# Prompt experts: ScalarE weights the V row, GpSimd adds it to a sum in SBUF, and the token rows stand in PSUM

## What is computed

```python
def peer_ffn(h, w_q, sub_keys, u_tab, v_tab):
    def one(hb):                       # a block of 128 tokens
        ...                            # scores against keys, the best 16 of each of 8 heads
        gate = jax.nn.softmax(best_s, axis=-1)
        act = jax.nn.gelu(jnp.einsum('thkd,td->thk', u_tab[idx], hb), approximate=False)
        return jnp.einsum('thk,thkd->td', gate * act, v_tab[idx])

x = x + g2 * peer_ffn(hff, ...)
```

## Time and profile before

| | |
|---|---|
| median of 3 runs | 4979.95 us (4967.22 to 4985.87) |
| the profiled execution | 4967.69 us |
| its span, first to last instruction | 4965.9 us |
| from the first dot of the prompt's slots to the last, within the span | 393 to 1103 us in layer 0, 2824 to 3529 us in layer 1 |

### The profile page before, as it was taken

How to read it: one execution, slowest core, us unless ns; L and a number is a source line. 1 busy time by engine, 2 the same in 40 slices (tenths; PEclk the granted TensorE clock), 3 DMA queues, 4 the chain that set the end, 5 groups by cost and what they waited for, 6 DMA issues and landing times. The chain is left out here.

```text
span 4965.9 us, 36487 instructions
## 1 busy us (share of the span) xinstructions
PE 3861.3 (78%) x11046; PEld 1898.0 (38%) x11046; DVE 3242.6 (65%) x8263; ACT 748.0 (15%) x2211; POOL 1447.9 (29%) x1284
## 2 busy tenths in 40 slices
PE   7588678988777776788868786788977687777776
PEld 6464334643222222235535443346422222222222
DVE  1546765536887868854574766664378787687666
ACT  0111124211101010010121112341010100100101
POOL 0001112212454434432222021221044354354432
PEclk9788788999999999999989897899999999999999
DMA  8334456754998999999969254566389899899998
GB/s 266 99 116 178 153 188 242 252 194 192 412 415 368 421 374 414 421 390 387 365 245 366 97 203 146 206 253 220 127 354 421 365 419 421 362 421 421 407 421 341
DMA packets 342149, 1497.72 MB, mean 302 GB/s; under 512 B 31424, under 2 KB 176448, under 8 KB 178112
## 3 DMA queue, kind: packets, MB, share of 16 engines
q0 software_dynamic: 184320, 1342.26, 67.4%
q1 hardware_dynamic: 157632, 153.13, 9.6%
HBM read 1491.97 MB, written 3.31 MB: 301 GB/s over the span
## 5 line engine op out<-in xcount | busy, mean ns | idle before, releaser
L680 PE MATMUL expert_acc<-uv_ring,diag 128*128 128x512 f32 x3744 | 1865.1, 631 | 417.9 <-DVE diag L1227 407.8
L634 POOL DMA_INDIRECT uv_ring<-uv,expert_index x936 | 1050.2, 1122 | 2717.1 <-PE expert_acc L680 2174.4
L680 PEld LDWEIGHTS expert_acc<-uv_ring,diag 128*128 128x128 f32 x3744 | 688.1, 198 | 1487.8 <-DVE diag L1227 898.5
L1218 DVE CUSTOM_DVE_ANT_0 uv_ring<-uv_ring,arena 128x1024 f32<-128x1024 f32 x680 | 831.5, 1223 | 243.2 <-DMA uv_ring<-uv,expert_index 240.5
L680 PE MATMUL expert_acc<-arena,diag 128*128 128x512 f32 x1376 | 687.8, 632 | 264.2 <-DVE diag L1227 196.3
L951 ACT ACTIVATE gelu<-u_dot 128x1 f32<-128x1 f32 x1280 | 256.0, 203 | 2943.8 <-DVE u_dot L1218 2943.2
L1227 DVE TENSOR_SCALAR diag<-const_mats,expert_gate,gelu 128x128 f32<-128x128 f32 x1280 | 465.7, 364 | 308.8 <-ACT gelu L951 214.1
L634 POOL DMA_INDIRECT arena<-uv,expert_index x344 | 397.6, 1156 | 757.2 <-PE expert_acc L680 460.3
L1218 DVE CUSTOM_DVE_ANT_0 arena<-arena 128x1024 f32<-128x1024 f32 x344 | 420.8, 1223 | 172.6 <-DMA arena<-uv,expert_index 171.2
L680 PEld LDWEIGHTS expert_acc<-arena,diag 128*128 128x128 f32 x1376 | 243.4, 195 | 698.1 <-DVE diag L1227 425.2
L1218 DVE CUSTOM_DVE_ANT_0 uv_ring<-uv_ring,prompt_rows 128x1024 f32<-128x1024 f32 x256 | 312.1, 1219 | 113.4 <-DMA uv_ring<-uv,expert_index 112.9
(11 more groups left out here) (202 smaller groups left out, 2785.0 us busy)
## 6 DMA issues: line engine op xcount, KB each, us to landing
w_ring<-w_ada SPq DMA_DIRECT2D x66, 512.0 KB, 11.3
w_ring<-w_in SPq DMA_DIRECT2D x64, 512.0 KB, 5.0
w_ring<-w_pq SPq DMA_DIRECT2D x64, 512.0 KB, 4.5
w_ring<-w_out SPq DMA_DIRECT2D x32, 512.0 KB, 6.3
uv_ring<-w_ada SPq DMA_DIRECT2D x30, 512.0 KB, 5.3
uv_ring<-uv,expert_index POOLq DMA_INDIRECT x936, 11.7
arena<-b_ada SPq DMA_DIRECT2D x48, 128.0 KB, 6.2
arena<-uv,expert_index POOLq DMA_INDIRECT x344, 15.7
```

Source lines behind the costliest of these rows:

```text
L634: pool.indirect_dma_start(out=UV[j], out_offset=None, in_=uv, in_offset=bass.IndirectOffsetOnAxis(ap=idxs[:, n % 2, k:k + 1], axis=0)).the ...
L680: ins = pe.matmul(acc[:, half, :], diag[:, m % DIAGS, :], UV[SLOT_AT[m]][:, D + 512 * half:D + 512 * half + 512], start=(k == 0), stop=(k ...
L1218: V_.tensor_tensor_reduce(UV[j][:, 0:D], UV[j][:, 0:D], rows_of(n), 1.0, 0.0, ALU.mult, ALU.add, dots[:, m % DOTS:m % DOTS + 1]).then_inc( ...
```

## The change

For the two prompt blocks only (`summed_by_pool(n)`, n = 0 and 5), steps 3 to 5 above are done by other engines:

- ScalarE, after the gelu, multiplies it with the gate (a 128x1 instruction), and then multiplies the whole v row of 1024 in place with that number (a 128x1024 instruction), at the same point of its program as the gelu.
- GpSimd adds the weighted row to `pool_sum` in SBUF, which it clears once at a block's start. In its queue the add of slot m - 5 stands ahead of the transfer of slot m, which takes the same buffer.
- VectorE makes no diagonal matrices and TensorE does no sums for these blocks.
- The two PSUM banks of `expert_acc`, which are free meanwhile, hold the prompt's token rows: TensorE transposes them there in one go after the prompt's scores (`rows_to_psum`), and VectorE's dot reads its second input from PSUM. The copy by ScalarE into `prompt_rows` is gone, and so is that tile.
- At the end VectorE takes `pool_sum` instead of the PSUM sum.

The blocks of the sample are as before. In the changed kernel lines are shifted: L680 is L715, L951 is L998, L634 is L666.

```diff
+def summed_by_pool(n):
+    return n % NBLK == 0
...
+        weight = sb("expert_weight", [P, DOTS])
-        htok_p = sb("prompt_rows", [P, D])
+        pacc = sb("pool_sum", [P, D])
...
+            def add_row(n, k):                      # gpsimd
+                m = n * SLOTS + k
+                if k == 0:
+                    if n:
+                        pool.wait_ge(s_pup.sem, n)
+                    nc.gpsimd.memset(pacc[:], 0.0).then_inc(pool_chain, 1)
+                    pool.wait_ge(pool_chain, sum(summed_by_pool(x) for x in range(n + 1)))
+                else:
+                    pool.wait_ge(s_vs, m)
+                pool.wait_ge(s_pw, sum(SLOTS for x in range(n) if summed_by_pool(x)) + k + 1)
+                nc.gpsimd.tensor_tensor(pacc[:], UV[SLOT_AT[m]][:, D:2 * D], pacc[:], ALU.add).then_inc(s_vs, 1)
...
+                            while summed_by_pool(n) and n * SLOTS + added <= SLOT_BEFORE[m]:
+                                add_row(n, added)
+                                added += 1
...
             def add_beside(n, m):                   # tensor
-                if 2 <= m <= SLOTS + 1:
+                if 2 <= m <= SLOTS + 1 and not summed_by_pool(n):
                     add_v(n, m - 2)
+            def rows_to_psum(n, b):
+                if n:
+                    if summed_by_pool(n - 1):
+                        pe.wait_ge(s_dot, n * SLOTS)
+                    else:
+                        pe.wait_ge(s_pup.sem, n)
+                for c in range(DC):
+                    ins = turn(acc[:, c // 4, (c % 4) * P:(c % 4 + 1) * P], hT[:, c, b * P:(b + 1) * P])
+                ins.then_inc(s_prow, 1)
...
+            def weigh(n, k):                        # scalar
+                m = n * SLOTS + k
+                act.wait_ge(s_gel, m + 1)
+                chain(nc.scalar.activation(weight[:, m % DOTS:m % DOTS + 1], gel[:, m % DOTS:m % DOTS + 1], ACT.Copy,
+                                           scale=gat[:, n % 2, k:k + 1]))
+                v = UV[SLOT_AT[m]][:, D:2 * D]
+                nc.scalar.activation(v, v, ACT.Copy, scale=weight[:, m % DOTS:m % DOTS + 1]).then_inc(s_pw, 1)
...
                 if m < SLOTS:                       # gelu_beside
                     gelu(n, m)
+                    if summed_by_pool(n):
+                        weigh(n, m)
...
             def rows_of(n):                         # vector
-                return htok[(n % NBLK - 1) % 2] if n % NBLK else htok_p[:]
+                return acc[:].rearrange("p a n -> p (a n)") if summed_by_pool(n) else htok[(n % NBLK - 1) % 2]
...
+                if summed_by_pool(n):               # add_peer
+                    chain(V_.tensor_tensor(pacc[:], pacc[:], G[:, gate_tile(n // NBLK, 1, g), :], ALU.mult))
+                    V_.tensor_tensor(X[:, n % NBLK, :], X[:, n % NBLK, :], pacc[:], ALU.add).then_inc(s_pup.sem, 1)
+                    return
...
-                if 1 <= m <= SLOTS:                 # dot_beside
+                if 1 <= m <= SLOTS and not summed_by_pool(n):
                     weigh(n, m - 1)
```

More of the change, by code:

```diff
@@ L174, with diag_turn @@
 SLOT_AT, SLOT_BEFORE, SLOT_TURN = slot_buffers()
+def summed_by_pool(n):
+    return n % NBLK == 0
+def diag_turn(n, k):
+    return sum(SLOTS for x in range(n) if not summed_by_pool(x)) + k
 class Beside:
@@ L267, in psum_order @@
             out += [("n2", l, g, i) for i in range(2 * nb)]
-            out += [("pq", l, g, i) for i in range(8)] + [(s, l, g, i) for s in ("ht", "ps") for i in range(2)]
+            out += [("pq", l, g, i) for i in range(8)] + [(s, l, g, i) for s in (("ht", "ps") if g else ("ps",)) for i in range(2)]
             out += [("pq", l, g, i) for i in range(8, 16)] + [("ps", l, g, 2), ("ps", l, g, 3)]
@@ L480, in build @@
         s_dg = ctx.enter_context(nc.semaphore("diag_ready"))
+        s_pw = ctx.enter_context(nc.semaphore("v_weighted"))
+        s_prow = ctx.enter_context(nc.semaphore("rows_in_psum"))
         s_vs = ctx.enter_context(nc.semaphore("v_summed"))
@@ L622, in _ @@
                         n = blk(l, g, b)
+                        added = 0
                         for k in range(SLOTS):
@@ L635, in _ @@
                                                     in_offset=bass.IndirectOffsetOnAxis(ap=idxs[:, n % 2, k:k + 1], axis=0)).then_inc(s_gat[j], 16)
+                        while summed_by_pool(n) and added < SLOTS:
+                            add_row(n, added)
+                            added += 1
         @block.tensor
@@ L677, in add_v @@
                     pe.wait_ge(s_pup.sem, n)
-                pe.wait_ge(s_dg, m + 1)
+                pe.wait_ge(s_dg, diag_turn(n, k) + 1)
                 for half in range(2):
-                    ins = pe.matmul(acc[:, half, :], diag[:, m % DIAGS, :], UV[SLOT_AT[m]][:, D + 512 * half:D + 512 * half + 512],
+                    ins = pe.matmul(acc[:, half, :], diag[:, diag_turn(n, k) % DIAGS, :], UV[SLOT_AT[m]][:, D + 512 * half:D + 512 * half + 512],
                                     start=(k == 0), stop=(k == SLOTS - 1), skip_group_check=True)
@@ L881, in score_block @@
                     def score_block(b, first=0, last=4):
-                        for half in range(0 if first else 2):
+                        for half in range(0 if first or not g else 2):
                             t = fill("ht", l, g, 2 * b + half)
@@ L910, in _ @@
                     if g == 0:
+                        rows_to_psum(blk(l, 0, 0), 0)
                         beside.start(blk(l, 0, 0), BESIDE_SAMPLE, {})
@@ L1122, in drain_scores @@
                                 act.wait_ge(s_dot, (blk(l, g, b) - 1) * SLOTS)
-                            nc.scalar.activation((htok[b % 2] if g else htok_p[:])[:, 512 * half:512 * half + 512], t, ACT.Copy).then_inc(free["ht"].sem, 1)
+                            nc.scalar.activation(htok[b % 2][:, 512 * half:512 * half + 512], t, ACT.Copy).then_inc(free["ht"].sem, 1)
                         for k in range(first, last):
@@ L1226, in weigh @@
                 dve.wait_ge(s_gel, m + 1)
[L1227 removed]
+                V_.tensor_scalar(diag[:, diag_turn(n, k) % DIAGS, :], C[:, C_ID, :], gat[:, n % 2, k:k + 1], gel[:, m % DOTS:m % DOTS + 1],
                                  ALU.mult, ALU.mult).then_inc(s_dg, 1)
@@ L1678, in _ @@
                     if g == 0:
-                        dve.wait_ge(*free["ht"].at(l, 0, 1))
+                        dve.wait_ge(s_prow, l + 1)
                         prompt_choice = choose(0)
```

3 lines of the change are left out of this document (1 added, 2 removed), and 2 rows, old and new, of the table FULL_COUNTS.

## The result

The changed kernel took 4995.48 us (median of 16 runs, 4987.05 to 5004.30), the kernel before 4980.74 (16 runs beside them). The ratio is 1.0031, with a 95% interval from 1.0022 to 1.0040: 15 us longer, where 34 less were forecast. That is less than the 0.5% which the prediction took for telling a change from none, but the interval leaves out 1: the kernel became longer, by little. The profiled one of before lies 13 us under its median and the one of after 1 us above, so about half of what the stages differ by in sum is the scatter of single executions. Only differences of many us in one stage are read.

The account below looks back on a forecast made before the run. No engine bounds all of it, so each stage was priced by itself: -12 + 20 + 8 + 5 + 3 - 23 - 18 = -17 us a layer, -34 in all, 4979.95 to 4946 us; range 4855 to 5060, forecast's own 4900 to 4990.

Parts of the forecast that it names:

- the hold: GpSimd's add stops VectorE's two-input work in SBUF; priced at the whole 2.29 us for each add that meets it.
- Heads, +5 forecast: Heads, 36 slots, per layer: small two-input VectorE sums caught behind adds, +5 us (bounds -8 and +33).
- The third rival: Heads: ScalarE bounds them, every second slot puts 1.5 us on the chain of exps; +27, 4990 us, chance 0.15.
- some 2 us come back: Heads, end of each block of four: TensorE's last products, formerly delayed by sums, regain some 2 us.
- Scan, +8 forecast: Scan, 8 steps per layer: ScalarE's slots replace TensorE's 3.7 us, each step 1 us longer; +8 (bounds -4 and +20).
- Turns and norms, +3: Short chains between stages, per layer: adds catching small instructions and TensorE's clock falling, +3 us (bounds 0 and +8).
- Taps, +20: Taps, per layer: 10 adds of 2.29 us stop VectorE, less 12 diagonals of 0.2; +20 us (bounds -3 and +38).
- Output projection -23: Output projection, 16 slots per layer: 5.17 us a tile falls to 3.7, bound by transfers; -23 us (bounds -2, -27).
- Query projection -18: Query projection, 13 slots per layer: 10.3 us a tile falls to 7.4 by transfers; -18 us (bounds 0 and -22).
- Input projection to taps -12: Input projection to taps, per layer: six TensorE sums (10.3 us) and 2 us of transfer waits go; bounds -5, -20.
- The first (no hold): Whole kernel: GpSimd doesn't hold VectorE, so -61 us a layer, 4858 us; chance 0.25.
- The second (the add far above 2.29 us): GpSimd becomes the bound in projections, then heads; with 4.1 us adds +84 a layer, 5148 us; chance 0.20.

## Why the prediction was wrong

The direction was wrong, and the step that failed is the price of the heads: the hold was put into +5 us there, and cost 18. The same fault is in the scan and the short chains. (The time, 4995 us, is within the stated 4855 to 5060 and 5 us above the forecast's own range.)

**Heads, +5 forecast, +28.9 measured.** The prediction took the hold for certain, but applied its 2.29 us in full only to the taps. In the heads it priced it as part of 5 us, since the instructions there are tiny. The runs show +18 us from the reads. The sums of one column there, duration min/median/max in ns, after:
```profile
L1610 DVE TENSOR_TENSOR stats<-stats x16: 149/208/2246, 832.4 to 987.0; 128x1 f32<-128x1 f32 x16
```
and with memsets for adds:
```profile
L1612 DVE TENSOR_TENSOR stats<-stats x16: 150/150/157, 786.4 to 923.9; 128x1 f32<-128x1 f32 x16
```
A held instruction lasts until the add's end, whatever its own length, and at worst through the end of the issue ahead too (2.98 us, L1581). Where another engine waits for it, gaps on VectorE do not absorb that. TensorE's waits for L1581 in the heads are 17.2 us; with memsets the same product (L1583) is waited for less:
```profile
PE rotating L697 <- DVE arena L1583: 5.8, 3, 1.9
```
So 11 us more in the change show in this wait alone; how the rest of the 18 adds up was not followed. The other 10 us are the weighting. The third rival (ScalarE bounds the heads, 4990 us) named that mechanism, at +27; its total is near the measured one by luck, for 18 of the 29 us lost in the heads are the hold. The relief, which the prediction partly credited ("some 2 us come back"), was nothing; the clock fell with it.

**Scan, +8 forecast, +17.7 measured.** The prediction had the weighting cancel TensorE's relief: measured -10.4 and +14.2. "L1444 behind an add" and its fellows were put at 1 us a step; the reads cost 11.3 in eight steps and GpSimd's time 2.6.

**Turns and norms, +3 and +12.9.** The bound of +8 was passed: again the hold, 10 of them.

**Taps, +20 and +8.7.** The hold was right: 10 adds by 2.29 us were forecast, 20.4 us measured. Too small was the relief, 0.2 us for each of 12 diagonals; without the added work the stage is 13 us shorter. The prediction said that VectorE runs without a pause there and that TensorE's relief is worth nothing; but in that stage VectorE is busy 77.78 of 95 us. Behind the taps it waits for small products of TensorE, which stand in its queue behind the sums. The same wait in the kernel before and in the one without the added work:
```profile
DVE arena L1384 <- PE rotating L753: 9.9, 4, 3.2
...
DVE arena L1446 <- PE rotating L799: 2.5, 1, 2.5
```
That is 7.4 us. A late transfer makes 2.1, and the diagonals, without which two dots in a row start 1.14 and not 1.40 us apart, 3.1 for twelve: 12.6 of the 13. So in this stage the hold was priced right, and the relief at a fifth of its size.

**Projections.** Output projection -23 and -21.2, with the first half of the slots 3.45 us apart, which is TensorE's tile, and the second half 3.61 (3.7 forecast). The size was right, but not by the transfers: the 3.61 is GpSimd, which the prediction had at 3.23 a slot; the 0.27 before an issue was missing, and the add was 0.1 longer. Without adds the slots stay 3.45 us apart, so the transfers bounded nothing at 3.7. Query projection -18 and -27.9: from the first dot (slot 115) to the last 17.2 us were gained, as forecast, but TensorE went on with sums for 7 us behind the last dot, and the forecast ended at it. In all TensorE loses some 16 sums there, 16 x 1.72 = 27.5 us, and after it has hardly a gap. Input projection to taps -12 and -6.4: by the table the relief is 17.7 us there, of which the weighting, GpSimd's time and its reads take back 1.8, 5.3 and 4.2. The late transfers stayed, 21.1 us of waiting where 19.3 were before:
```profile
DVE uv_ring L1276 <- DMA uv_ring<-uv,expert_index: 21.1, 4, 5.8
```

**Rivals.** The first (no hold) would have been 4858 us; the run with GpSimd's reads taken away, 4868, stands for that kernel. Its condition was false, and its price came near in part by luck: it had the heads at -2 and the scan at -3 a layer, where that run shows +11 and +6, and the taps at -3 and the query projection at -18, where it shows -12 and -29. It was also argued for with no instruction of VectorE being long because of an issue. Four diagonals beside an issue in the first block are, by a little (0.50 us, not 0.34):
```profile
802.16 0.50 DVE L1227 TENSOR_SCALAR diag<-const_mats,expert_gate,gelu 128x128 f32<-128x128 f32 x1 [1.66 <-ACT gelu L951]
```
The second (the add far above 2.29 us) is out, at 2.39. Of the signs named beforehand, the add, the weighting and the output projection's dots came out, and GpSimd was busy 67% of the heads. The taps' 115 us did not (103), nor the scan's 17.5 us a step (18.7).

The Trainium skill, "SBUF — State Buffer", section "SBUF: two separate sides", has a VectorE instruction with two SBUF inputs contend only against a GpSimd instruction that reads SBUF. The trace agrees: 11.48 us for ten taps beside adds, 7.21 beside memsets. The fault was not the rule but where its price was put.

## What to carry to other kernels

Before work is moved to GpSimd, list every VectorE instruction with two SBUF inputs that lies in a chain, however small, and charge each that can meet GpSimd's instruction with the rest of that instruction; then see whether one operand can come from PSUM. Move the work stage by stage: here the same edit gave 21 us in one stage and cost 29 in another, and split by stage it turned 0.3% slower into 2% faster. Look at the granted clock of an engine that was relieved: in the heads it fell from 0.95 to 0.59 and the relief gave back nothing. And look at what stands behind the removed work in the queue: here TensorE's small products behind the taps came earlier, which nobody had counted.

## What the runs showed of the hardware

- GpSimd and VectorE exclude each other in both directions when VectorE has two inputs in SBUF and GpSimd's add reads SBUF: VectorE's instruction of one column took 2.25 us (0.15 alone), GpSimd's add 2.78 (2.35 alone). An instruction of VectorE that begins during the issue ahead of an add is held until the add's end (2.98 us, 0.16 alone). The dot with one input in PSUM takes 1.215 us beside adds and 1.220 before, with no adds.
- An indirect issue of GpSimd is held by a dot with both inputs in SBUF (1.98 us beside 0.95), and not by one with an input in PSUM (0.95).
- Memsets of GpSimd held none of the taps, products or sums. One exception in each prompt block was an in-place multiply-add of 4 columns with a single input (L1251): it began during an issue and took 2.61 us, until the end of the three memsets behind it. Its cause is open.
